# Reordering the attention stage of a decoder step: result copies, roots, softmax weights, the new tokens' product and the last head's gate

## The reference

```python
# layer A, for prompt and samples
b, c, h, z = split(rms_norm(x) @ w_in_a)
x = x + (b * conv3_causal(c * h) * silu(z)) @ w_out_a
k, v = split(rms_norm(x) @ w_kv);  k = rope(rms_norm(k))
# layer B
q, z = split(rms_norm(x) @ w_in_b);  q = rope(rms_norm(q))
p = softmax(q k^T / sqrt(128))               # two per head
o = (p[0] - lambda * p[1]) @ v               # past and new tokens, causal
x = x + (rms_norm(o) * (1 - lam_init) * silu(z)) @ w_out_b
```

## Time and profile before

| | us |
|---|---|
| median of 3 runs | 2563.27 (2562.97 to 2569.68) |
| the profiled execution | 2559.86 |
| its span | 2558.1 |
| TensorE busy | 2465.2 (96% of the span) |
| VectorE, ScalarE, GpSimd busy | 1432.5, 1077.8, 355.3 |
| DMA | 520.54 MB, mean 203 GB/s |

### The profile page before, as it was taken

One profiled execution on the slowest core, in us unless ns is written; L12 is line 12 of the kernel. 1 busy time (PEld: TensorE's weight loads), 2 busy tenths in 40 slices (PEclk: granted clock), 3 DMA queues, 4 the chain that ended last, 5 costly groups with the idle time before them and its releaser, 6 DMA issues.

```text
span 2558.1 us, 51073 instructions
## 1 busy us (share of the span) xinstructions
PE 2465.2 (96%) x20963; PEld 2165.3 (85%) x20963; DVE 1432.5 (56%) x1635; ACT 1077.8 (42%) x1896; POOL 355.3 (14%) x137
## 2 busy tenths in 40 slices
PE   8999999999999999999999999999899978789999
PEld 7999999999999999899999889999788833345655
DVE  5665565565665334455676778787672256652211
ACT  4111111121121223777877778787454234441111
POOL 4323333333321111000000000000000012230000
PEclk9999999999999999999999999999999989989999
DMA  5323323232322332334588887788788789989995
GB/s 155 84 82 99 82 82 98 82 82 82 98 82 87 104 113 88 104 104 156 174 310 316 285 298 278 248 294 305 264 296 300 256 324 390 377 302 360 341 336 218
DMA packets 373255, 520.54 MB, mean 203 GB/s; under 512 B 16553, under 2 KB 311858, under 8 KB 354610
## 3 DMA queue, kind: packets, MB, share of 16 engines
q1 hardware_dynamic: 314434, 461.55, 52.6%
q10 hardware_dynamic: 58528, 56.45, 6.4%
q0 software_dynamic: 128, 0.26, 0.0%
HBM read 483.46 MB, written 34.75 MB: 203 GB/s over the span
## 4 chain that ended last, share of the span: by engine, by line
PE 83%; ACT 5%; DMA 4%; DVE 4%; issue 2%; SPq 1%; POOL 1%; ACTq 0%; DVEq 0%; POOLq 0%
PE psum L117 25%; PE psum L1441 16%; PE psum L125 12%; PE psum L1449 8%; PE psum L2076 7%; PE psum L955 4%; PE psum L1492 3%; DMA w_raw<-in_w_in_b_dram 2%; ACT w_raw L1189 2%; DVE h_keys_turned L1379 2%; PE psum L1457 1%; PE psum L2126 1%; PE psum L2107 1%; ACT w_hi L1205 1%; DMA w_raw<-in_w_in_a_dram 1%
## 5 line engine op out<-in xcount | busy, mean ns | idle before, releaser
L1441 PE MATMUL psum<-x_hi,w_hi 128*128 128x272 f32 x2048 | 433.1, 292 | 0.0
L117 PE MATMUL psum<-x_hi,w_hi 128*128 128x272 f32 x2048 | 427.1, 289 | 2.2 <-DVEq L451 2.2
L117 PE MATMUL psum<-x_lo,w_hi 128*128 128x272 f32 x2048 | 426.2, 290 | 0.0
L1441 PE MATMUL psum<-x_lo,w_hi 128*128 128x272 f32 x2048 | 424.6, 288 | 0.0
L1441 PEld LDWEIGHTS psum<-x_hi,w_hi 128*128 128x128 f32 x2048 | 320.3, 188 | 22.1 <-issue 22.1
L1379 DVE STREAM_TRANSPOSE h_keys_turned<-h_ring 128x1024 f32<-128x1024 f32 x256 | 300.2, 1216 | 50.5 <-DMA h_ring<-in_cache_k_dram 33.5
L117 PEld LDWEIGHTS psum<-x_hi,w_hi 128*128 128x128 f32 x2048 | 321.6, 189 | 2.7 <-issue 2.3
L117 PEld LDWEIGHTS psum<-x_lo,w_hi 128*128 128x128 f32 x2048 | 320.9, 188 | 0.0
L1441 PEld LDWEIGHTS psum<-x_lo,w_hi 128*128 128x128 f32 x2048 | 320.4, 188 | 0.0
L404 POOL TENSOR_TENSOR w_raw<-w_raw,params 128x2048 f32<-128x2048 f32 x63 | 247.8, 3934 | 500.6 <-DMA w_raw<-in_w_in_a_dram 500.6
L1449 PE MATMUL psum<-x_hi,w_lo 128*128 128x272 f32 x2048 | 289.6, 296 | 0.0
(11 more groups left out here) (229 smaller groups left out, 3039.2 us busy)
## 6 DMA issues: line engine op xcount, KB each, us to landing
h_ring<-in_cache_k_dram SPq DMA_DIRECT2D x256, 512.0 KB, 7.1
h_ring<-in_cache_v_dram SPq DMA_DIRECT2D x103, 1024.0 KB, 7.1
w_raw<-in_w_in_a_dram SPq DMA_DIRECT2D x64, 1024.0 KB, 6.4
w_raw<-in_w_kv_dram SPq DMA_DIRECT2D x16, 2048.0 KB, 11.9
w_raw<-in_w_in_b_dram SPq DMA_DIRECT2D x15, 2048.0 KB, 8.5
h_keys_turned<-in_cache_v_dram SPq DMA_DIRECT2D x25, 1024.0 KB, 7.0
w_raw<-in_w_out_a_dram SPq DMA_DIRECT2D x16, 1024.0 KB, 5.7
wo_raw<-in_w_out_b_dram SPq DMA_DIRECT2D x8, 2048.0 KB, 11.9
```

What stands on the lines that cost most here:

```text
L117: pe.matmul(out[:, g, 0:GT], m.WH[s][:, k * P:(k + 1) * P], x[:, k * T + g * GT:k * T + (g + 1) * GT], start=(k == 0 and x is xh), stop=Fa ...
L1441: pe.matmul(psum[n % 2][:, g, 0:GT], m.WH[n % 2][:, k * P:(k + 1) * P], x[:, k * T + g * GT:k * T + (g + 1) * GT], start=(k == 0 and x is ...
```

## The change

- The step table: for sequences 3 to 7 max, turn, diag, spread, shift, exp and sum stand one page later and the weights one page earlier; for sequence 2 the weights stand one page earlier. `LAST_NORM` moves the turning of sequence 1's rows from page 33 to 34.
- ScalarE: at a sequence's first page the row copy comes first; the roots (`norm_o`), `split_y`, `split_hi(0)` and `split_hi(1)` come behind everything else of their page; the softmax steps come behind the head's own.
- `first_new` and `add_first_new` move from page 27 to page 30.
- The last head is gated by VectorE (three operations) in place of GpSimd, and `split_lo(1)` comes behind them.
- At the start of `project_and_score` block 0 is squared ahead of `scale_pair(1)`.

```diff
@@ project_and_score, ScalarE @@
             for n in range(N):
                 if n >= 1:
                     square(n - 1)
+                if n == 1:
+                    scale_pair(1)
...
-                if n % 2 == 0 and n + 2 < N:
+                if n and n % 2 == 0 and n + 2 < N:
                     scale_pair(n // 2 + 1)
@@ attend_and_project @@
-    LAST_NORM = 1
+    LAST_NORM = 2
...
             if i == 1:
-                return dict(max=6, turn=9, diag=9, spread=10, shift=10, exp=11, sum=12, sums=13, weights=14, group=15)
-            return dict(max=2, turn=4, diag=5, spread=6, shift=7, exp=8, sum=9, sums=11, weights=13, group=14)
+                return dict(max=6, turn=9, diag=9, spread=10, shift=10, exp=11, sum=12, sums=13, weights=13, group=15)
+            return dict(max=3, turn=5, diag=6, spread=7, shift=8, exp=9, sum=10, sums=11, weights=12, group=14)
@@ GpSimd @@
-            for r in range(H):
+            for r in range(H - 1):
                 gate(r)
@@ ScalarE @@
                 if j == 4:
                     prompt_weights(r, 1)
                     prompt_exps(r, 3)
-                    if r:
-                        norm_o(r - 1)
...
-                if j == 8:
-                    if r + 1 < H:
-                        prompt_exps(r + 1, 0)
-                    if r:
-                        split_y(r - 1)
-                    if r == H - 1:
-                        split_hi(0)
+                if j == 8 and r + 1 < H:
+                    prompt_exps(r + 1, 0)
+
+            def slow_step(v):
+
+                r, j, n, q = place(v)
+                if r is not None:
+                    if 4 in parts_at(j) and r:
+                        norm_o(r - 1)
+                    if 8 in parts_at(j):
+                        if r:
+                            split_y(r - 1)
+                        if r == H - 1:
+                            split_hi(0)
+                elif n == 0:
+                    if q == 0:
+                        norm_o(H - 1)
+                        split_hi(1)
+                    if q == 1:
+                        split_y(H - 1)

             def block_step(n, j):
                 if j == 0:
                     if n == 0:
                         square_o(H - 1)
-                        norm_o(H - 1)
-                    split_hi(n + 1)
-                if j == 1 and n == 0:
-                    split_y(H - 1)
+                    else:
+                        split_hi(n + 1)
...
-                if p == 0 and i:
-                    soft.take_rows(act, i - 1)
...
             for v in range(V0, NV):
                 r, j, n, q = place(v)
-                seq_step(v // NPG, v % NPG)
+                if v and v % NPG == 0:
+                    soft.take_rows(act, v // NPG - 1)
+                    slow_step(v - 1)
                 if r is not None:
                     for k in parts_at(j):
                         head_step(r, k)
                 else:
                     block_step(n, q)
+                seq_step(v // NPG, v % NPG)
+                if v % NPG != NPG - 1:
+                    slow_step(v)
@@ VectorE @@
+            def gate_last():
+
+                dve.wait_ge(gate_in, H * 16)
+                dve.wait_ge(o_ln, H * 2)
+                o3 = o[H - 1].rearrange("p (e t) -> p e t", e=2)
+                dve.tensor_tensor(o3, o3, ro[H - 1].unsqueeze(1).to_broadcast([P, 2, SEQ]), ALU.mult).then_inc(normed, 1)
+                dve.wait_ge(normed, H)
+                dve.tensor_tensor(o[H - 1], o[H - 1], zh, ALU.mult).then_inc(y_ready, 1)
+
+            def gate_low():
+
+                dve.wait_ge(yh_ready, H)
+                at = slice((H - 1) * 2 * SEQ, H * 2 * SEQ)
+                dve.tensor_tensor(yl[:, at], o[H - 1], yh[:, at].bitcast(F32), ALU.subtract).then_inc(yl_ready, 1)
...
-                if j == 1:
+                if n == 0 and j == 1:
+                    gate_last()
+                if n == 0 and j == 2:
+                    gate_low()
+                if j == (2 if n == 0 else 1):
                     split_lo(n + 1)
@@ VectorE, and the same on TensorE before first_new @@
-                if v == V0 + 5:
+                if v == V0 + HP + 1:
                     soft.add_first_new(dve)
```

## The result

| | median us | runs | ratio to before (95% interval) | profiled execution | its span |
|---|---|---|---|---|---|
| before | 2564.11 | 6 | | 2559.86 | 2558.1 |
| changed | 2546.48 | 6 | 0.9929 (0.9914 to 0.9943) | 2546.37 | 2544.6 |
| changed, measured again | 2548.26 | 6 | 0.9936 (0.9918 to 0.9954) | 2547.76 | 2545.7 |

The change makes the kernel 16 to 18 us faster, not the 25.8 of the sum. The profiled executions differ by 13.5 only; the one of before was a fast one, 4 us under its median. The time lies inside the forecast range of 2526 to 2551, but 9 us above the forecast of 2537.5 and nearer to the 2541 to 2542 of three rivals (transfers bind, the weights still meet GpSimd, the last gate is late). None of the three is what happened, as traces and experiments show, so the number alone would have misled.

What follows compares the result with a forecast made beforehand. TensorE, busy 96% of the span, was the bound, with its waits and the slow clock behind them to win; DMA was the heads' second bound. 1.6 + 16.5 + 7.7 = 25.8 us gave a median of 2537.5, range 2526 to 2551.

Steps and rivals of the forecast that it cites:

- the sum: Whole kernel: 1.6 for block 0, 16.5 for the heads and 7.7 for output block 0, together 25.8 us.
- transfers bind: Rival, from head 1 on: DMA limits the heads to 10 to 14 us instead of 16.5; 2541.5; chance 0.19.
- the weights still meet GpSimd: Rival, head 5: softmax weights shifted into GpSimd's gate of head 4, 3.7 to 5.5 us less gain; 2542; chance 0.09.
- the last gate is late: Rival, output block 0: VectorE's gate ends after 2287, TensorE waits, 3 to 4 us less gain; 2541; chance 0.04.
- Block 0 of the projections: Start of projections: squaring first starts the sum earlier; gain 1.6 us, between 1.4 and 5.7, with a new 3.6 wait.
- Head 0: New tokens' product moved to head 1: its 8.57 us wait goes; net gain 8.1 us, between 5 and 11.
- Head 5: Weights a page earlier, copy ahead of grouping: the 7.0 us wait and 2.2 of slow product go, 9.2.
- Output block 0: First output block: row copy earlier removes a 4.81 us page wait and slow products; gain 7.7, between 4.8 and 8.2.
- Result copies: Heads 1, 2, 4, 6: moved softmax steps delay copies 0.9 each, minus 3.6; with head 2's 1.1, minus 2.5.
- The slower rival: Five heads (0, 1, 2, 4, 6): copies wait for a step and a blocked operation, 7.1 each; 2573; chance 0.03.
- transfers just allow it: DMA over the heads: the 16.5 us gain fits 14.3 of idle DMA time plus 2.2 out of the ring.
- The rivals on transfers: Heads: transfers bind from head 1 on (2541.5, chance 0.19), or are at a ceiling already (2554, chance 0.05).

Runs made afterwards that it cites:

- e1: Kernel before with only the new tokens' product and its addition moved to head 1 (page 30): 2555.4 us, ratio 0.9970.
- e5: Kernel before with only ScalarE's order changed (result and row copies ahead of roots, high parts and weight splits): 2549.79 us, ratio 0.9939.
- e7: Changed kernel with the whole table of softmax pages as before, weights included: 2536.72 us, ratio 0.9891.
- e11: Changed kernel with GpSimd's two gate multiplications of every head 0 to 6 cut from 1024 columns to 8: 2530.67 us, ratio 0.9869.
- second trace: The changed kernel run again without edits, beside the later experiments: 2548.26 us, ratio 0.9936.
- e2: Changed kernel with softmax steps of sequences 3 to 5 back at their old pages, weights kept at page 12: 2535.37 us, ratio 0.9885.
- e8: e2 with the second sequence's sum at page 13, its product and weights at 14, behind the result copy: 2533.95 us, ratio 0.9876.
- e6: Changed kernel with the last head's gate back on GpSimd and the second low weights split back at page 79: 2549.49 us, ratio 0.9935.
- e3: Changed kernel with GpSimd's two gate multiplications for head 3 cut from 1024 columns to 8: 2543.27 us, ratio 0.9922.
- e4: Kernel before with only the second weight pair's scaling moved behind the first square in the projections: 2563.52 us, ratio 0.9999.

## Why the prediction was right, and where not

**Block 0 of the projections**: right at its place. From the landing of the weights (line 1189) to the second low product 22.65 us before and 21.03 after: 1.6 forecast, 1.6 measured, with the new wait (4.64, forecast 3.6) and slow matmuls behind it. What reaches the head start can't be told. From the landing to page 22 the three traces with the old order take 1019.3 to 1020.4 us, the eleven with the new one 1016.4 to 1021.4 (mean 1018.8): between stands the stage with the cached keys, where TensorE waits some 20 us for turned keys.

**Head 0**: 8.1 forecast, 7.6 in the first trace, 5.0 in the second, 7.7 alone (e1). The wait for the values is gone in both, so the mechanism is right; that the first trace comes so near the figure is in part luck. The second lost 3 us between product 0 and 1, where it waits 2.36 us for the copy like the first (2.35) but has the scores behind at half speed (2.93 against 1.56). Over all traces the stretch takes 59.0 to 63.1 with the product at its old place (three) and 48.2 to 54.5 at its new one (eleven).

**Head 5**: 8.3 with the copy's share, 8.2 in the trace. e5 shows the mechanism: the copy ahead of the grouping, whatever the weights do. The 2.4 us in the stretch behind are what the weights' new page leaves there, a gain that the sum left out (29.0 and 28.9 with the weights late in e5 and e7, 24.1 with the new page, 26.5 before).

**Output block 0**: 7.7 forecast, 6.6 measured. The page wait and its slow matmuls are gone, but the block starts 4.05 us late for the high part of its weights (2.07 before), behind GpSimd's gate of head 6; with that gate cut to 8 columns the wait is 1.36 and product 7 to the end 287.7 (e11). The product ahead of it ends sooner and that chain doesn't.

**Result copies: the step that failed**, with the heads 3 and 7 and, for the diagonal, head 4. The sum had minus 2.5 for all moved softmax steps: 0.9 for each copy, since the product's 4.58 us "cover the mix and part of it", and nothing for turn, diagonal, spreading and shift, which have no term. Measured with copies and diagonal: product 1 to 3 3.0 us worse than forecast, 3 to 4 6.0, 6 to 7 2.8 (2.3, 6.5 and 0.3 in the second trace). With the steps back (e2) product 1 to 3 gains 2.9, against 2.8 that the sum had there without its copies: the rest of that row was right. The copies alone, in the four heads that the term names (1, 2, 4, 6), cost TensorE waits of 1.44, 3.77, 0.34 and 2.25 us where 0.34 each is the least in any trace: 6.4 us in place of 3.6; the diagonal's 4.3, which has no term, comes on top. Two errors are in the term. First, I looked at VectorE's steps by their own durations and at the end of each head only, while GpSimd's gate multiplies from 2120.08 to 2124.88, around the start of head 2's product, and holds VectorE there; a moved step is late by the hold too, and with it all that queues behind. Second, moving `spread` by a page puts a wait into TensorE's own queue: its release, the diagonal, then fell inside the gate. The order of the instructions showed both neighbours; I costed only the softmax weights against the gate. The slower rival did hold the mechanism (a copy behind "a whole step (1.9) and a blocked operation (2.2)"), but asked for it in five heads; it came in full in one (head 2, 3.77 us), in part in heads 0, 1 and 6 (2.35, 1.44, 2.25; the sum had 2.2 for head 0), in head 4 not at all (0.34, as with the steps back), and beside it the diagonal's, which it didn't have.

The Trainium skill (SBUF — State Buffer, Who interferes with whom) lists `tensor_scalar` among the VectorE operations that can, if their operands allow it, contend with GpSimd for the pair of ports that the two share, and says that whoever issues first keeps the pair for a whole instruction. I had used its sentence on operations with two SBUF inputs alone. The traces agree with the list: lines 1962, 881 and 1968, all tensor_scalar, end with GpSimd's instruction or 0.3 us behind it (2.21, 2.18, and 2.62 in e2), and the reduction from PSUM between them (line 880) takes its usual 0.31.

**DMA**: "transfers just allow it" held. The heads and the first gap behind them, page 22 to the first output matmul, took 221.9 us before, 215.8 after, 205.0 in e2, 203.3 in e8 and 201.7 in e11: up to 20 us less, against 16.5 from idle time and ring. In e11 the engines are at 1.02 to 1.03 and 415 to 424 GB/s from 2152 to 2230, so there the second bound is near. The rivals on transfers are refuted by e2, and that on a late VectorE gate by the traces, in which TensorE never waits for the low part, with either gate (e6); that the weights meet GpSimd in head 5 didn't happen: they end at 2201.5 there and the gate begins at 2202.76.

## What to carry to other kernels

A step that is moved must be laid beside everything that its engine shares, not only beside its own queue: find the stretches in which GpSimd works on SBUF, and keep out of them what another engine waits for, however small (a 0.17 us operation cost 2.2). Where several parts of a change are measured at once, a gain can hide a loss of nearly the same size: undoing the table of pages alone brought another 11 to 13 us, beside the 16 to 18 of the whole change. And before explaining a few us between two traces, look how far two executions of the same instructions lie apart up to that place.

## What the runs showed of the hardware

- A tensor_scalar on 128x2 elements took 0.17 us alone and 2.21 beside a 2.34 us tensor_tensor of GpSimd on SBUF; with the latter cut to 8 columns it took 0.17 again (e3). What it costs is what is left of GpSimd's operation when it starts: 2.21, 2.07, 1.42 and 1.07 us for starts 0.15, 0.32, 0.97 and 1.30 us behind GpSimd's, in the changed kernel.
- The landing of the second pair of q weights varied from 1024.8 to 1028.9 us over the fourteen traces, whatever the edit behind it: chance of that size stands ahead of everything that is compared here.
- The length of a wait of some 2 us doesn't settle the clock behind it. In head 0 the changed kernel waits 1.93 us ahead of a turn and goes on at full speed; e2, with the same instructions there, waits 2.47, and the scores behind it run at half of it. At the same place the page behind a wait of 1.89 (e4) and 1.99 (e3) took 1.90, behind 2.18 (e5) and 2.22 (e6) it took 1.04. Scores for 512 columns, the changed kernel's, then e2's; with the page beside it (1.90 against 1.04), two turns and the longer wait it makes the 3.1 us:

```profile
2065.42 1.88 PE L2140 MATMUL psum<-heads 128*128 128x512 f32 x4
...
2066.93 3.28 PE L2140 MATMUL psum<-heads 128*128 128x512 f32 x4
```

- The DMA engines moved 424 GB/s over 25 us on this one core (e11).
